# A two-layer diffusion trunk on one core: keys, scores and head sums of the mixer put in another order, head norms on other engines

## The reference

```python
hx, hc = _mlstm_bidir(qx, kx, vx, gx, qc, kc, vc, gc, need_ctx)
ml_x = (_head_norm(hx, ml_norm_w) * jax.nn.sigmoid(ox.astype(f32))).astype(ux.dtype)
na_x, na_c = _neighbourhood_attention(nqx, nkx, nvx, nqc, nkc, nvc, rpb, need_ctx)
yx = jnp.concatenate([ml_x, na_x], -1) @ w_out

def _mlstm_outputs(q, k, v, log_i, log_f, incoming):
    ...
    s = jnp.einsum('bhcjk,bhcsk->bhcjs', qc, kc) * jnp.exp(dmat - m_j[..., None])
    inter = jnp.exp(m_inter - m_j)
    num = jnp.einsum('bhcjs,bhcsv->bhcjv', s, vc) + inter[..., None] * jnp.einsum('bhcvk,bhcjk->bhcjv', c_in, qc)
    den = s.sum(-1) + inter * jnp.einsum('bhck,bhcjk->bhcj', n_in, qc)
    h = num / jnp.maximum(jnp.abs(den), jnp.exp(-m_j))[..., None]

def _head_norm(h, w):
    mu = h.mean(-1, keepdims=True)
    var = jnp.square(h - mu).mean(-1, keepdims=True)
    return _merge_heads((h - mu) * lax.rsqrt(var + LN_EPS)) * w
```

## Time and profile before

| | us |
|---|---|
| median of 3 runs | 4182.33 |
| lowest, highest | 4179.69, 4194.31 |
| the profiled execution | 4179.24, of which 4177.4 are its span |
| busy in the span | PE 3591.4, DVE 2774.5, POOL 1852.7, ACT 1698.1 |
| mean granted TensorE clock | 0.976 of full speed |

### The profile page before, as it was taken

The page is one execution under the profiler, slowest core; times in us unless marked ns, Lnnn a source line. Parts: engine busy times, 40 slices in busy tenths (PEclk is TensorE's granted clock), DMA queues, the critical chain, the costliest instruction groups (busy, mean ns, idle before and its releaser), DMA issues.

```text
span 4177.4 us, 46868 instructions
## 1 busy us (share of the span) xinstructions
PE 3591.4 (86%) x12376; PEld 1566.1 (37%) x12376; DVE 2774.5 (66%) x6948; ACT 1698.1 (41%) x4782; POOL 1852.7 (44%) x1429
## 2 busy tenths in 40 slices
PE   7999899888888888898787787889988888888886
PEld 3445554433333333333211112555433333333332
DVE  3204767777767777777767665578777777777774
ACT  2012515444444444444444443343444444444443
POOL 1100115556556556555433332113555555655564
PEclk8999899999999999999999998899999999999999
DMA  7642249999999999999999997437999999999997
GB/s 285 236 168 51 106 192 416 421 421 421 421 419 415 415 418 419 414 418 412 419 419 412 411 410 306 114 149 290 421 421 421 422 419 417 419 413 415 411 421 329
DMA packets 244586, 1496.45 MB, mean 358 GB/s; under 512 B 25648, under 2 KB 44592, under 8 KB 73632
## 3 DMA queue, kind: packets, MB, share of 16 engines
q0 software_dynamic: 191232, 1385.58, 80.7%
q1 hardware_dynamic: 53152, 108.50, 7.5%
HBM read 1487.57 MB, written 2.21 MB: 357 GB/s over the span
## 4 chain that ended last, share of the span: by engine, by line
DMA 45%; PE 26%; DVE 9%; issue 9%; ACT 6%; POOL 5%; SPq 0%; POOLq 0%; DVEq 0%; ACTq 0%; PEldq 0%
DMA arena<-in_updown,arena 43%; PE psum L1156 8%; POOL arena L1709 4%; DVE arena L2214 4%; PE psum L1099 3%; PE psum L945 2%; PE psum L961 2%; PE psum L967 1%; ACT arena L1523 1%; ACT arena L1519 1%; PE psum L1232 1%; ACT L1572 1%; PE psum L1126 1%; ACT L1508 1%; PE psum L1013 1%
## 5 line engine op out<-in xcount | busy, mean ns | idle before, releaser
L1709 POOL DMA_INDIRECT arena<-in_updown,arena x1280 | 1754.8, 1371 | 1729.7 <-PE psum L1156 823.7
L1156 PE MATMUL psum<-arena 128*128 128x512 f32 x4096 | 1994.6, 616 | 338.7 <-ACT arena L1523 320.4
L2214 DVE CUSTOM_DVE_ANT_0 arena<-arena 128x1024 bf16<-128x1024 f32 x1276 | 1566.1, 1227 | 901.7 <-DMA arena<-in_updown,arena 793.5
L1156 PEld LDWEIGHTS psum<-arena 128*128 128x128 f32 x4096 | 711.6, 190 | 1393.2 <-ACT arena L1523 834.7
L1572 ACT ACTIVATE arena<-arena 128x1 f32<-128x1 f32 x1280 | 259.2, 203 | 1666.4 <-DVE arena L2214 1663.7
L1523 ACT ACTIVATE arena<-CN,arena 128x128 f32<-128x128 f32 x1280 | 514.0, 402 | 44.9
L1232 PE MATMUL psum<-arena 64*64 64x512 f32 x2048 | 291.3, 640 | 137.2 <-ACT arena L1523 136.7
L1519 ACT ACTIVATE arena<-arena 128x1 f32<-128x1 f32 x1280 | 377.0, 295 | 66.2 <-ACT arena L1572 2.6
L1126 PE MATMUL psum<-arena 128*128 128x256 f32 (+1 forms) x1280 | 363.1, 384 | 3.0 <-ACT arena L1494 1.6
L1126 PEld LDWEIGHTS psum<-arena 128*128 128x128 f32 x1280 | 238.8, 190 | 260.8 <-issue 253.0
L1232 PEld LDWEIGHTS psum<-arena 64*64 64x64 f32 x2048 | 54.6, 135 | 326.6 <-ACT arena L1523 314.7
(11 more groups left out here) (235 smaller groups left out, 2732.0 us busy)
## 6 DMA issues: line engine op xcount, KB each, us to landing
arena<-in_ada_w POOLq DMA_DIRECT2D x40, 1024.0 KB, 6.0
arena<-in_updown,arena POOLq DMA_INDIRECT x1280, 14.7
arena<-in_wq SPq DMA_DIRECT2D x16, 1024.0 KB, 19.0
arena<-in_w_in SPq DMA_DIRECT2D x48, 256.0 KB, 7.3
arena<-in_w_in SPq DMA_DIRECT2D x5, 2048.0 KB, 12.0
arena<-in_w_in SPq DMA_DIRECT2D x18, 512.0 KB, 5.2
arena<-in_ada_w SPq DMA_DIRECT2D x4, 2048.0 KB, 14.3
arena<-in_bias SPq DMA_DIRECT2D x16, 512.0 KB, 5.0
```

The source lines that it names most:

```text
L1156: mm = e.matmul(ps[ACCUMULATORS[t % 2][hf]][:], diag[:, k % DIAGS, :], ring[k % RING][:, D + hf * 512:D + (hf + 1) * 512], start=first, st ...
L1709: e.indirect_dma_start(ring[k % RING], None, updown, bass.IndirectOffsetOnAxis(ap=idx16[:, k:k + 1], axis=0)).then_inc(sem(f"rows{k % RING ...
L2214: e.tensor_tensor_reduce(prod[:, k % 2, :], ring[k % RING][:, 0:D], u, 1.0, 0.0, ALU.mult, ALU.add, dots[:, k:k + 1]).then_inc(sem("expert ...
```

## The change

1. Keys and scores: in layer 0 the fifth tile is turned and scored in the middle of the fifth B job, the sixth after it, so that nothing stands behind the last job but the states. VectorE takes the last weighings, applications and both `scale_q` before the last job is emptied. In layer 1 the third set stands in the middle of the second B job; ScalarE takes all decays and pair exponents in one row, and both B jobs are emptied by VectorE. `scale_q` of layer 1 moves two states back.
2. Head sums go by tile: `head_sums(g)` takes the two heads of a pair for one tile, the two 128-row products first, then the two 64-row ones, which lie in the two halves of the rows.
3. Head norms: ScalarE takes the root of each tile as it is done (`head_roots`), VectorE its reciprocal and a shift (`shift`), ScalarE scales and shifts the heads (4 operations, `head_norm`), and GpSimd multiplies by the gates (`gate_heads`), after it has multiplied the gates by the norm's weights once. The two first normalisations of attention stand ahead of the last `head_rows`.
4. SyncE in layer 1: K0 goes to a fourth place (`nk`, in two transfers), and K1, K2, K3 are issued ahead of the maxima. `wb1`, the weights of the B jobs, goes ahead of the bands' transfers. Three halves of the bias are loaded early and five after the sums; in layer 1 `w_out` is loaded two pairs later.

```diff
     for t in range(NCT) if l else list(range(NCT, NT)) + list(range(NCT)):
-        jobs.append(("B", t, "x", "va"[t % 2]))
...
         assert (NT - NCT) * 512 <= 4 * T
 
+        def chunk_slot(l, n):
...
+                    if chunk_user(l, n) is not None:
+                        e.wait_ge(sem("mixer.proj_mm"), chunk_end(jobs, order[chunk_user(l, n)]))
+                    slot = chunk_slot(l, n)
+                    if slot == 3:
+                        for b in range(2):
+                            e.dma_start(nk[:, :, b * P:(b + 1) * P], wv[:, b:KD:2, col:col + P]).then_inc(sem("mixer.wch_loaded3"), 16)
...
+                    if l and n == 3:
+                        e.dma_start(wb1, wv[:, :, COL_NV:COL_NV + 512]).then_inc(sem("mixer.wtok_loaded1"), 16)
                         e.wait_ge(sem("mixer.proj_mm"), last_job(jobs, "G"))
                         place_bands(vlat1)
-                        e.dma_start(wb1, wv[:, :, COL_NV:COL_NV + 512]).then_inc(sem("mixer.wtok_loaded1"), 16)
...
+                    if l == 0 and n == 3:
+                        store_negm()
+                if l:
+                    store_negm()
+                    e.wait_ge(sem("mixer.negm_stored"), 32)
+                    e.wait_ge(sem("mixer.proj_mm"), last_job(jobs, "V"))
+                    load_negm(0)
+                    load_negm(1)
+                    load_pairs(0)
+                    load_pairs(1)
...
+                for n in range(3):
+                    load_bias(n)
...
+                for n in range(3, 2 * NBAND):
                     load_bias(n)
-                if l:
-                    e.wait_ge(sem("mixer.nmax_ready"), 4)
-                    load_wo()
                 e.wait_ge(sem("mixer.nmax_ready"), 6)
-                load_bias(7)
                 if l == 0:
                     e.wait_ge(sem("mixer.mlT"), NT)
-                    load_wo()
+                load_wo()
...
+                def keys_and_scores(x):
+
+                    if l and x == 0:
+                        turn_k(TURN_TILES[0])
+                        turn_k(TURN_TILES[1])
+                    turn_k(TURN_TILES[x + t0])
+                    tile_scores(t0 + x)
...
+                            if k == KD // 2 and n - first_job(jobs, "B") == (1 if l else 4):
+                                keys_and_scores(2 if l else 4)
...
-                            tile_scores(b)
+                            if b < 5:
+                                keys_and_scores(b if b < 4 else 5)
...
+                            for x in range(2):
+                                keys_and_scores(x)
                         else:
-                            for t in TURN_TILES[2:]:
-                                turn_k(t)
-                            tile_scores(NCT + 2)
-                            tile_scores(NCT + 3)
+                            keys_and_scores(3)
...
+                def head_sums(g):
+
...
+                    if g >= 2:
+                        e.wait_ge(sem("mixer.h_done"), 2 * g - 2)
...
+                        slot = inter_slot(l, d, j)
+                        outs = [ps[4 + 2 * (g % 2) + o][:, d * (DV + 1):(d + 1) * (DV + 1)] for o in range(2)]
+                        for o in range(2):
+                            mm = e.matmul(outs[o], decay[l][d][:, 2 * o + c, j * P:(j + 1) * P], vml[:, j, 2 * c + o, :], start=True, stop=slot is None)
+                        for o in range(2 if slot is not None else 0):
+                            rows = slice(o * DK, (o + 1) * DK)
+                            mm = e.matmul(outs[o], qe_of[l][d][rows, c, slot * P:(slot + 1) * P], states[rows, c, d, scan_place(d, j) - 1, :], start=False, stop=True)
+                    mm.then_inc(sem("mixer.num_ready"), 2)
...
+                        e.wait_ge(sem("mixer.h_done"), MLH * (NT - t0) - 2)
...
+                        for p in range(2):
+                            for d in range(2):
+                                decays(d, p)
+                        for d in range(2):
+                            pair_exps(d)
...
-                exponent(0)
-                exponent(1)
-                e.wait_ge(sem("mixer.h_done"), MLH * (NT - t0))
-                e.wait_ge(sem("eps_set"), 1)
-                e.activation(rstd[:, t0 * MLH:], stat[:, t0 * MLH:, 1], ACT.Sqrt, bias=epsc[:, 0:1]).then_inc(sem("mixer.hsd"), 1)
...
+                    e.wait_ge(sem("mixer.h_done"), MLH * (t - t0 + 1))
+                    e.activation(rstd[:, t * MLH:(t + 1) * MLH], stat[:, t * MLH:(t + 1) * MLH, 1], ACT.Sqrt, bias=epsc[:, 0:1]).then_inc(sem("mixer.hsd"), 1)
...
+                    e.wait_ge(sem("mixer.shift_ready"), t - t0 + 1)
+                    for h in range(MLH):
+                        n, w = t * MLH + h, H[:, t, h * DV:(h + 1) * DV]
+                        ins = e.activation(w, w, ACT.Identity, scale=rstd[:, n:n + 1], bias=shifts[:, n:n + 1])
+                    ins.then_inc(sem("mixer.normed"), 1)
+
+                for t in range(t0, NT):
+                    if t == NT - 1:
+                        exponent(0)
+                        exponent(1)
+                    head_roots(t)
+                    if t > t0:
+                        head_norm(t - 1)
+                head_norm(NT - 1)
...
+                def gate_heads(t):
...
+                    e.tensor_tensor(H[:, t, :], H[:, t, :], sigo[:, t, :], ALU.mult).then_inc(sem("mixer.mlout"), 1)
...
+                for t in range(t0, NT):
+                    e.tensor_tensor(sigo[:, t, :], sigo[:, t, :], nwrow, ALU.mult)
+                e.wait_ge(sem("mixer.masks_loaded"), 16)
+                for n in range(3):
+                    add_masks(n)
+                for t in range(t0, NT - 1):
+                    gate_heads(t)
+                for n in range(3, 5):
+                    add_masks(n)
+                gate_heads(NT - 1)
+                for n in range(5, 2 * NBAND):
+                    add_masks(n)
...
-                        if b >= 2:
+                        if 2 <= b <= 4:
                             apply(b - 2)
+                        if b == 4:
+                            weigh_k(4)
+                            apply(3)
+                            scale_q(0)
+                        if b == 5:
+                            weigh_k(5)
+                            apply(4)
+                            apply(5)
+                            scale_q(1)
                     if l and kind == "B" and i == 1:
-                        weigh_k(0)
-                        weigh_k(1)
+                        for x in range(4):
+                            weigh_k(x)
+                        apply(0)
+                        apply(1)
+                        weigh_k(4)
+                        apply(2)
                     if ev != "v":
                         continue
...
-                for x in range(2 if l else NT - 1, NT):
-                    weigh_k(x)
-                for x in range(0 if l else NT - 2, NT - t0):
-                    apply(x)
+                if l:
+                    weigh_k(5)
+                    apply(3)
                 for x in range(2 * STATES):
                     keep_state(x)
-                    if x in (3, 5):
-                        scale_q(x // 2 - 1)
...
+                def shift(t):
+
+                    e.wait_ge(sem("mixer.hsd"), t - t0 + 1)
+                    r = rstd[:, t * MLH:(t + 1) * MLH]
+                    ch.link(e.reciprocal(r, r))
+                    e.scalar_tensor_tensor(out=shifts[:, t * MLH:(t + 1) * MLH], in0=stat[:, t * MLH:(t + 1) * MLH, 0], scalar=-1.0, in1=r,
+                                           op0=ALU.mult, op1=ALU.mult).then_inc(sem("mixer.shift_ready"), 1)
...
-                for p in range(len(pairs) + 3):
-                    if 1 <= p < len(pairs):
+                groups = 2 * (NT - t0)
+                for g in range(groups):
+                    if g == groups - 1:
+                        normalise(0)
+                        normalise(1)
+                    head_rows(g)
+                    if g >= 3 and g % 2 == 1:
+                        shift(t0 + (g - 3) // 2)
+                    if g == groups - 2:
+                        e.wait_ge(sem("mixer.bands_placed"), 16 * BAND_DMAS)
+                        e.wait_ge(sem("mixer.num_ready"), MLH * (NT - t0))
+                        ch.link(e.memset(no_bias, 0.0))
+                        find_max(0)
+                for p in range(1, len(pairs) + 3):
+                    if p < len(pairs):
                         find_max(p)
-                    if 1 <= p <= len(pairs):
+                    if p == 1:
+                        shift(NT - 1)
+                    if 2 <= p <= len(pairs):
                         normalise(2 * p - 2)
                         normalise(2 * p - 1)
-                    k = mlstm_tile_at(p, 1, NT - t0)
-                    if k is not None:
-                        head_norm(t0 + k)
```

161 lines of the change are left out of this document (71 added, 90 removed).

## The result

The changed kernel took 4142.14 us (median of 4 executions, 4133.81 to 4144.19) against 4181.01 for the kernel before; the ratio is 0.9895, with a 95% interval from 0.988 to 0.9911. The profiled execution took 4144.19 us, 35.1 less than the profiled one before. The forecast was 4138 in a range from 4122 to 4162, so the time is in the range and the sign is right. The sum behind it is less so: three of its six terms are off by 4 to 7 us, in both directions.

A forecast was written before the change was run, and what follows sets the result against it. In the two mixers the bound was taken to change from VectorE to TensorE and back. Gains of 8.9 + 12.1 + 15.2 + 8.3 = 44.5 us took the profiled 4179.24 to 4134.7, median 4138, range 4122 to 4162.

The forecast's parts named there:

- Layer 0, up to the first sum: Layer 0's value jobs to first head sum: VectorE's work lies under the last job, first sum 3.8 us earlier.
- Layer 0, sums: Layer 0's head sums: VectorE becomes the bound, last row done 42.8 us after the start; 8.9 us with the step before.
- The rival in which GpSimd shuts VectorE out: Attention normalisations each wait for a whole mask operation, 6 us in each layer: 4150; chance 0.05.
- The low clock in these sums: Rival in layer 0's head sums: three groups at 4.3 us and slow scores, 7 us: 4145; chance 0.22.
- Layer 0, attention: Layer 0's attention: six head norms leave VectorE, the seventh pair's turn comes at t+27.5, 12.1 us gained.
- Layer 1, to the first sum: Layer 1's jobs to first head sum: K3's weights issued ahead of the maxima, tail 10.4 us; 12.9 us gained.
- Layer 1, sums: Layer 1's head sums: start at the low clock, 4.3 us a group, last 38.0 us; 15.2 us with the step before.
- Layer 1, attention: Layer 1's attention: as layer 0 with four tiles, sixth pair's turn at t+23.8 against 32.1, 8.3 us gained.
- pairs without overlap: Rival in the head sums: 64-row pairs do not overlap, a pass stays 0.21 us: 4152; chance 0.09.
- the unchanged period of attention: Rival in attention: the loop through three engines sets the period, 20.4 us less gain: 4158; chance 0.12.
- slower: Rival in attention: idle stretches before the second pair leave TensorE at 1.2 GHz throughout, up to 4254; chance 0.03.
- layer 1's sums at the high clock throughout: Rival in layer 1's head sums: they keep the high clock, 6 us more gain: 4132; chance 0.06.

The follow-up runs named there:

- the first profiled execution: The changed kernel as first measured, nothing altered; this profiled execution took 4144.19 us.
- the second execution: The same changed kernel run once more, nothing altered; the profiled execution took 4133.79 us, the median of five was 4132.65 us.
- the slower course: Four of the unaltered changed kernel's nine executions, 4141.9 to 4144.2 us; the other five took 4129.9 to 4133.8 us.
- the experiment: Changed kernel with head norms back on VectorE, one root for all tiles, no shifts and GpSimd on masks alone: 4143.93 us.
- layer 0's keys behind the last job: Changed kernel with two mask halves before the gates, and layer 0's keys, scores and VectorE tail work put back as before: 4136.15 us.
- the semaphores cleared early: Changed kernel with VectorE clearing the previous stage's semaphores in layer 1 while waiting for the first value job: 4136.46 us.
- the maxima first: Changed kernel with SyncE's store and loads of the maxima in layer 1 put ahead of the last key chunk again: 4148.44 us.
- the longer one: Changed kernel with eight extra mask-sized sums at the head of GpSimd's row of 12 in layer 0: 4151.68 us, one execution.
- the kernel with the last tile's norm later: The fastest kernel with the last tile's root and norm behind the second pair's exponents, its shift behind that pair's normalisations: 4131.19 us.
- the masks' move: Changed kernel with GpSimd adding masks to two halves of the bias before the gates instead of three: 4132.06 us.
- the fastest kernel: Changed kernel with two mask halves before the gates, and semaphores cleared in layer 1 behind an early projection: 4128.63 us.

## Why the prediction was right, and where its steps were wrong

**Where the gain lies** was right: only in the two mixers, and there where the windows said that VectorE or a transfer is late.

**Layer 0, up to the first sum**: 3.8 forecast, 3.45 measured in every trace with this part, and 3.44 lost when it was taken out. Right; the start of the states and of the sums shows 0.73 and 1.32 us put down to issue, which I had not counted in full.

**Layer 0, sums**: the term was 5.1 us for the sums themselves; it was minus 1.9 in the first profiled execution and 8.8 in the second. Two steps failed. The first is the price of a pass: I took 0.21 us for 128 rows and 0.085 for 64, counting that only the 64-row pairs gain, and they are 0.16 and 0.107 at the high clock, so that a group is 2.14 and not 2.35 us. The row of VectorE is 2.62 and not 2.78 us, and the first is there 1.6 us after the start, not 2.6. With the high clock up to TensorE's last sum, 42.8 us became 39.0, in the second execution. The second is that I looked for GpSimd's hold on VectorE in the wrong place. The rival in which GpSimd shuts VectorE out priced it at one mask operation for each normalisation of attention, 6 us a layer; there the lengthening was small, with 0.49 to 0.76 us for a normalisation. It struck a 4-column operation that I had costed at 0.16 us, for a whole row of operations, and cost 2.5 us itself and 6.5 through TensorE's clock. The low clock in these sums, the most likely rival at 0.22, came too, but not as described: it was high for the first two groups and half of the third, fell just ahead of the scores, rose, and fell again behind the shift. Its price of 7 us and the time of 4145 fit the slower course (4144.19) by the size of the sum alone. The length of the gap ahead of the sums, from which I had taken the level, did not decide it: the gap was 1.32 us in both executions. I had also misread the old rows. Before, the first passes behind the gaps of 2.93 and 2.59 us ran at the high clock (four of 128 rows in 0.68 us, two in 0.46 us), and the clock fell about a microsecond later.

**Layer 0, attention**: 12.1 forecast, 11.8 and 11.9 measured. The steps hold one by one: the second pair's turn came 8.1 us after find_max(1) (8.1 forecast), the third's 12.9 (12.9), the period was 3.70 (3.64). By the experiment the norms' place is worth 9.9 of it, before the 1.9 that the shifts cost in the sums.

**Layer 1, to the first sum**: 12.9 forecast, 7.8 and 8.3 measured. The part for the chunk is right (10.7 us by undoing it), and so is the end of the last job. The tail was forecast with 10.4 us and took 14.8. What failed is the list of what stands in it: the clearing of semaphores, 3.03 us, is not in the sum, because it has no row of its own in the kernel before, where a wait for the last job hid it, and because in the code it is one call. I had moved work behind it without asking what it costs when the cover is gone. The 4.02 us for which TensorE then idled brought it to the low clock in the states, 1.7 more, and GpSimd beside the first scaling made another 1.0. With all of it away the tail was 9.1 us.

**Layer 1, sums**: 2.3 forecast, 6.0 measured. Of the 3.7 between them 2.1 came up to the end of the first two attention scores, 14.2 us instead of 16.3, mostly by the price of a pass: at the low clock a group took 3.77 and not 4.3 us. The other 1.6 came behind them, where VectorE's rows are shorter than forecast as in layer 0. **Layer 1, attention**: 8.3 forecast, 8.3 and 8.1 measured.

So the total of 44.5 us was near the measured ones (35.1 and 45.5 by the profiled executions) with terms that were too small by 3.8 and 3.7 us in the sums, too large by 5.1 in layer 1's tail, and without the 10.7 us that separate the two profiled executions. That these cancel to 2 us in the second execution, and that 4138 lies between the two courses, is luck and not the working of the sum. Of the rivals, pairs without overlap fell, since undoing the order cost 20 us, and so did the unchanged period of attention, slower, and layer 1's sums at the high clock throughout (their first six half groups take 1.87 us each). That last one is real all the same: it came in the profiled execution with layer 0's keys behind the last job, and gave 5.3 us of the 6 that I had priced it with.

## What to carry to other kernels

When a change moves work behind a call that the profile before hides under a wait, price that call first: a row that isn't there is not a row of zero length. Before a tiny operation that reads two tensors out of SBUF is put on VectorE beside a long row of GpSimd's, write it with one tensor input and per-partition scalars. Here that costs 0.4 us more, and the longest wait of the other form was 8.5. It is shown not to wait for the operation in hand; in the place where the other form waited out the row only a reciprocal with one input was seen to run (0.14 us). And in a row of small matmuls group those of the same number of rows, with neighbours in different halves: one loop's order was worth 20 us of 4150, its effect on the clock included, and no engine had less to compute.

## What the runs showed of the hardware that was not expected

**A held operation can wait out a row.** The 4-column operation took 2.94, 3.23 and 2.89 us beside a row of 12 mask operations of 0.68 us (the changed kernel, the semaphores cleared early, the maxima first), and 8.52 us beside the longer one. Each of the four was issued in the eighth operation of the row and ended with the row. Issued in the sixth, it got in at the next boundary, after 0.40 to 0.67 us, in the four traces where that was so (one with a row of 12, three with a row of 8); and a later one, issued in the fourth of 12 in the kernel with the last tile's norm later, after 0.32. The Trainium skill, "SBUF — State Buffer", Who interferes with whom, says that whoever issues first has the shared ports for the whole instruction; the waits over many boundaries are longer than that. What decides between the two is open: no run here held all else still and moved only the shift. All four executions that waited also had the early fall of the clock (382.4 to 383.0), which in the first put the shift 1.6 us later; the four with the shift in the sixth operation had none there.

**The clock can differ at the same activity.** In two executions of one program TensorE was busy 3.59 of 5 us, with the same idle stretches of 0.73, 1.32 and 1.41 us, and then ran at 0.66 in one and at 1.00 in the other. Counted from the first sum, the busy times of the two agree to 0.02 us up to the fall. What the clock goes by in that place is not in the trace. Layer 1's sums got different clocks as well (29.04 us in one kernel's execution and 34.34 in another's, with the same code for that layer), but there the states ahead of them had already run differently, in 7.44 and 6.29 us. Whether the masks' move also helps in an execution with the fall at 383 isn't shown, since no profiled execution of that kernel had one. By an estimate it would: a row of 8 in place of 12 would have ended at 392.0 in the first execution (386.50 and eight of 0.68 us), 0.2 us after the shift was issued. The four times of that kernel (4131.7, 4132.0, 4132.2 and 4137.5 us) and those of the fastest kernel (4126.2, 4126.7, 4130.6 and 4131.8) would fit two courses some 5 us apart instead of 10, which is also the size of that difference in layer 1's sums.

**A pass has three prices**: 0.21, 0.16 and 0.107 us on average for the same 129 columns at the same clock, by what its neighbours are. It is the change between 128 and 64 rows that costs, some 0.2 us once, whichever bank is written.
